# Pacing the bias transfers, moving copies of products, and dividing a tile's four weight differences between GpSimd and VectorE

## What is computed

```python
def swiglu(h, wg, wu, wd):
    return (jax.nn.silu(h @ wg) * (h @ wu)) @ wd

for layer in range(DEPTH):                      # DEPTH = 2, D_MODEL = 1024, D_FF = 2816
    h = rmsnorm(x, ffn_norm_g[layer, 0])
    x = x + 0.5 * swiglu(h, ffn_w_gate[layer, 0], ffn_w_up[layer, 0], ffn_w_down[layer, 0])
    h = rmsnorm(x, mix_norm_g[layer])
    x = x + (gla_ssd_mixer(h, ...) if layer % 2 == 0 else dsa_mixer(h, ..., rel_bias))
    h = rmsnorm(x, ffn_norm_g[layer, 1])
    x = x + 0.5 * swiglu(h, ffn_w_gate[layer, 1], ffn_w_up[layer, 1], ffn_w_down[layer, 1])
return rmsnorm(x, final_norm_g)

# dsa_mixer: score[q, s] = sum over 16 heads of relu(q_idx . k_idx) * w_idx; the top 128 keys are kept;
# logits = q . kv / sqrt(128) + rel_bias[t5_bucket(distance)]; softmax; times kv; out projections
```

## Time and profile before

| | us |
|---|---|
| median of 3 runs (2090.89 to 2091.29) | 2090.96 |
| the profiled execution | 2087.45 |
| its span | 2085.6 |

### The profile page before, as it was taken

How to read it: one execution, slowest core, us unless ns; L and a number is a source line. 1 busy time by engine, 2 the same in 40 slices (tenths; PEclk the granted TensorE clock), 3 DMA queues, 4 the chain that set the end, 5 groups by cost and what they waited for, 6 DMA issues and landing times.

```text
span 2085.6 us, 34512 instructions
## 1 busy us (share of the span) xinstructions
PE 2036.5 (98%) x13775; PEld 1775.9 (85%) x13775; DVE 1558.3 (75%) x2293; ACT 1017.7 (49%) x1597; POOL 537.0 (26%) x431
## 2 busy tenths in 40 slices
PE   7999999999999999999999999999699999999998
PEld 6899998788888887999998899999565678999997
DVE  7777776595777898777776877776479857877775
ACT  5444444453445455444445544444267755544444
POOL 0334330001000002333420333342217412334330
PEclk9999999999999999999999999999899999999999
DMA  5333334332253423333323333334910112333332
GB/s 154 93 110 102 97 105 106 91 93 72 61 142 92 91 82 92 111 92 110 104 85 98 105 108 92 111 102 87 156 42 20 42 56 86 102 112 92 102 91 71
DMA packets 325284, 196.06 MB, mean 94 GB/s; under 512 B 14891, under 2 KB 317110, under 8 KB 325126
## 3 DMA queue, kind: packets, MB, share of 16 engines
q1 hardware_dynamic: 322502, 184.21, 30.5%
q0 software_dynamic: 2624, 9.67, 3.2%
HBM read 191.07 MB, written 2.79 MB: 93 GB/s over the span
## 4 chain that ended last, share of the span: by engine, by line
PE 63%; DVE 5%; DMA 2%; issue 2%; POOL 2%; ACT 1%; DVEq 0%; ACTq 0%; POOLq 0%
PE ps L1993 9%; PE ps L1995 9%; PE ps L1994 9%; PE ps L2058 4%; PE ps L2057 4%; PE ps L2059 4%; PE ps L1872 3%; PE ps L1871 3%; PE ps L1873 3%; DMA w_raw<-in_ffn_w_down 2%; PE ps L2565 1%; PE ps L2536 1%; POOL index_scores L541 1%; PE ps L2515 1%; PE ps L2078 1%
## 5 line engine op out<-in xcount | busy, mean ns | idle before, releaser
L1027 DVE TENSOR_TENSOR w_lo<-w_raw,w_hi 128x1024 fp32r<-128x1024 f32 (+1 forms) x351 | 425.7, 1213 | 72.3 <-ACT w_hi L563 72.2
L563 ACT ACTIVATE w_hi<-w_raw 128x1024 fp32r<-128x1024 f32 (+1 forms) x351 | 361.6, 1033 | 229.3 <-PE ps L1873 110.0
L472 POOL TENSOR_TENSOR sq<-w_raw 128x512 f32<-128x512 f32 x72 | 96.6, 1342 | 953.0 <-DMA w_raw<-in_ffn_w_up 923.5
L1995 PE MATMUL ps<-h_hi,w_lo 128*128 128x256 f32 x864 | 244.5, 283 | 0.0
L1993 PE MATMUL ps<-h_hi,w_hi 128*128 128x256 f32 x864 | 244.2, 283 | 0.0
L2057 PE MATMUL ps<-act_hi,w_hi 128*128 128x512 f32 x512 | 200.0, 391 | 0.0
L2058 PE MATMUL ps<-act_lo,w_hi 128*128 128x512 f32 x512 | 200.0, 391 | 0.0
L2059 PE MATMUL ps<-act_hi,w_lo 128*128 128x512 f32 x512 | 199.2, 389 | 0.0
L1993 PE MATMUL ps<-s_hi,mix_hi 128*128 128x256 f32 x576 | 164.4, 285 | 10.9 <-issue 8.2
L1993 PEld LDWEIGHTS ps<-h_hi,w_hi 128*128 128x128 f32 x864 | 165.6, 192 | 2.7
L1995 PEld LDWEIGHTS ps<-h_hi,w_lo 128*128 128x128 f32 x864 | 165.6, 192 | 0.0
(11 more groups left out here) (409 smaller groups left out, 5367.3 us busy)
## 6 DMA issues: line engine op xcount, KB each, us to landing
w_raw<-in_ffn_w_gate SPq DMA_DIRECT2D x88, 512.0 KB, 3.8
w_raw<-in_ffn_w_up SPq DMA_DIRECT2D x88, 512.0 KB, 3.8
w_raw<-in_ffn_w_down SPq DMA_DIRECT2D x64, 512.0 KB, 3.4
w_raw<-in_hy_w_in SPq DMA_DIRECT2D x44, 512.0 KB, 3.8
w_raw<-in_ffn_w_down SPq DMA_DIRECT2D x32, 384.0 KB, 3.5
w_raw<-in_hy_w_out SPq DMA_DIRECT2D x16, 512.0 KB, 3.9
acum_rows<-acum_scratch POOLq DMA_DIRECT2D x4, 1024.0 KB, 10.5
bias_rows<-line_scratch POOLq DMA_DIRECT2D x8, 512.0 KB, 24.0
```

The costliest lines, as they stand in the source:

```text
L563: act.activation(w_hi[:, s, 0:width[n]], w_raw[:, s, 0:width[n]], ACT.Copy).then_inc(hi_ready, 1)
L1027: dve.tensor_tensor(w_lo[:, s, 0:width[n]], w_raw[:, s, 0:width[n]], w_hi[:, s, 0:width[n]].bitcast(F32), ALU.subtract).then_inc(lo_ready, 1)
L1995: mm = pe.matmul(dst, wl, rh[:, k, :], start=False, stop=k == 3, skip_group_check=True)
```

## The change

Four edits. On GpSimd, `weight_sums` keeps the first two differences of a tile; the two that depend on them are made by VectorE in the new `last_weight_sums`, called for tile 4 after `scaled(1)` and for tile f + 1 after `product(f - 1)`. In mix1 the causal mask is made first, and bias transfer j waits until PE has finished unit `UB["mix1"] - 2 + j` by count: the first for down unit 5 (of 0 to 7), the second and third for 6 and 7, the others for mix1's units 0 to 4. On ScalarE, `keep(f, 0)` moves ahead of `s_high(3)`, `act_high` and `t_high` in tile 4, and ahead of `act_high` in tile 21. In ffn0 alone, `rms_out` and `silu(0)` on ScalarE and `scaled(0)` on VectorE move forward, the first ahead of the eight scaled copies of x and `scaled(0)` ahead of `h_sums`.

```diff
@@ gpsimd, weight_sums and mix1
                 pool.tensor_tensor(up[:, 0:HC], up[:, HC:UC], up[:, 0:HC], ALU.subtract).then_inc(t_made, 1)
-                pool.wait_ge(t_made, 4 * k + 1)
-                pool.tensor_tensor(mix_raw[:, HC:2 * HC], up[:, HC:UC], mix_raw[:, 0:HC], ALU.subtract).then_inc(t_made, 1)
-                pool.wait_ge(t_made, 4 * k + 3)
-                pool.tensor_tensor(mix_raw[:, 2 * HC:3 * HC], gate[:, HC:UC], mix_raw[:, HC:2 * HC], ALU.subtract).then_inc(t_made, 1)
...
-                for j, p0 in enumerate(range(0, P, SKEW)):
-                    lines = bass.AP(tensor=line_dram.tensor, offset=P - 1 - p0, ap=[[LINE - 1, SKEW], [SKEW * LINE, AH], [1, TOK]])
-                    pool.dma_start(bias_rows[p0:p0 + SKEW, :, :], lines).then_inc(pool_landed, 16)
-                pool.dma_start(w_uv_sb[:, :, :], a["dsa_w_uv"][0].rearrange("h c d -> c h d")).then_inc(pool_landed, 16)
                 pool.memset(causal_neg[:, :], 0.0).then_inc(a_cneg, 1)
                 pool.wait_ge(a_cneg, 1)
                 pool.affine_select(out=causal_neg[:, :], in_=causal_neg[:, :], compare_op=ALU.is_ge, fill=MASKED,
                                    base=0, pattern=[[-1, P]], channel_multiplier=1).then_inc(a_cneg, 1)
+                for j, p0 in enumerate(range(0, P, SKEW)):
+                    pool.wait_ge(unit_used, UB["mix1"] - 2 + j)
+                    lines = bass.AP(tensor=line_dram.tensor, offset=P - 1 - p0, ap=[[LINE - 1, SKEW], [SKEW * LINE, AH], [1, TOK]])
+                    pool.dma_start(bias_rows[p0:p0 + SKEW, :, :], lines).then_inc(pool_landed, 16)
+                pool.dma_start(w_uv_sb[:, :, :], a["dsa_w_uv"][0].rearrange("h c d -> c h d")).then_inc(pool_landed, 16)
                 pool.wait_ge(a_cneg, 2)
@@ scalar, ffn
                 act.wait_ge(x_upd, XB[st])
+                if st == STAGES[0]:
+                    rms_out(st)
                 for k in range(KT):
                     act.activation(s_raw[:, k, :], x[:, k, :], ACT.Copy, scale=gains[:, GAIN[st] + k:GAIN[st] + k + 1]).then_inc(s_hi_ready, 1)
                 produce_hi(n + 4)
-                rms_out(st)
+                if st == STAGES[0]:
+                    silu(0)
+                else:
+                    rms_out(st)
                 s_high(0)
                 s_high(1)
-                silu(0)
+                if st != STAGES[0]:
+                    silu(0)
...
+                    produce_hi(nxt_unit)
                     if f == PLAIN:
+                        keep(f, 0)
                         s_high(3)
-                    produce_hi(nxt_unit)
+                    elif f - 1 == LAST + 4:
+                        keep(f, 0)
                     act_high(f - 1)
                     if f < FT - 1:
                         t_high(f + 1)
-                    keep(f, 0)
+                    if f != PLAIN and f - 1 != LAST + 4:
+                        keep(f, 0)
@@ vector, ffn
+                def last_weight_sums(f):
+                    u, k = gate_unit(st, f), kb + f - PLAIN
+                    gate, up = w_raw[:, u % SLOTS, :], w_raw[:, (u + 1) % SLOTS, :]
+                    dve.wait_ge(t_made, 4 * k + 2)
+                    dve.tensor_tensor(mix_raw[:, HC:2 * HC], up[:, HC:UC], mix_raw[:, 0:HC], ALU.subtract).then_inc(t_made, 1)
+                    dve.wait_ge(t_made, 4 * k + 3)
+                    dve.tensor_tensor(mix_raw[:, 2 * HC:3 * HC], gate[:, HC:UC], mix_raw[:, HC:2 * HC], ALU.subtract).then_inc(t_made, 1)
...
+                if st == STAGES[0]:
+                    scaled(0)
                 h_sums()
                 produce_lo(n + 4)
                 s_low(0)
-                scaled(0)
+                if st != STAGES[0]:
+                    scaled(0)
...
                 scaled(1)
+                last_weight_sums(PLAIN)
                 product(1)
...
                     product(f - 1)
+                    if f < FT - 1:
+                        last_weight_sums(f + 1)
```

## The result

| | before | after |
|---|---|---|
| median, us | 2091.02 (2090.89 to 2091.29, 4 runs) | 2056.2 (2054.79 to 2056.34, 4 runs) |
| ratio to before | 1 | 0.983, 95% interval 0.9815 to 0.9849 |
| profiled execution, us | 2087.45 (span 2085.6, clock 0.994) | 2056.34 (span 2054.5, clock 1.000) |
| PE busy, us | 2036.5 (98%) | 2029.2 (99%) |
| VectorE busy, us | 1558.3 (75%) | 1555.1 (76%) |

The change is faster, by 34.8 us between the medians and by 31.1 us between the two profiled executions; the forecast was 25.75.

What follows compares the result with a forecast made beforehand. TensorE was taken as the bound, so gains lie only where it waits. Terms -22.25 + 5 - 3.0 - 4.2 - 1.3 = -25.75 us, off the median 2090.96, gave 2065.2 us; range 2057 to 2076.

Steps and rivals of the forecast that it cites:

- the bias additions: GpSimd's 16 causal-mask additions in mix1 end late and delay the weighted sum at L536: +5 us, ends 0 and 10.
- the basis: Whole kernel: the summed gain of 25.75 us, from the profiled 2087.45, was taken off the median 2090.96.
- The tail of ffn2: Last gate row to norm: pacing bias transfers stops them starving down weights, so it runs as in ffn1: -22.25 us.
- rival (a): In mix1 the bias additions are hidden after all and their 5 us fall away: 2059 us; chance 0.22.
- The product copies: ScalarE's earlier copies cut PE's waits at product 3: -3.0 us in tile 21, -4.2 in tile 4.
- the new stall: In tile 4 PE's wait moves from product 3 to product 5: about 1.45 us, in ffn0 1.9.
- The weight differences: FFN tiles: moving two of GpSimd's four differences to VectorE costs 0 for 72 tiles.
- the room: VectorE in a steady FFN tile: 2.5 us of its 3.77 us idle can be used before PE notices.
- ahead of an FFN's first such tile: VectorE waits up to 2.9 us for GpSimd there, but PE wants the queued work later: cost 0.
- Rival (d): VectorE becomes the bound of the FFN tiles, +53 us: 2118; decides from 2.5 us more per tile; chance 0.05.
- The start of ffn0: Moving rms_out and scaled(0) forward ends PE's wait for the gate row: -1.3 us, 3.4 as the far end.

Runs made afterwards that it cites:

- the control: The changed kernel itself, run again unaltered beside the second group of experiments: 2056.30 us, ratio to before 0.9841.
- the burst put back: The changed kernel with all eight bias transfers issued at once again, at the point where they were: 2078.36 us, ratio to before 0.9950.
- the late burst: The changed kernel with all eight bias transfers issued at once, but only when down unit 5 of ffn2 is done: 2063.36 us, ratio to before 0.9870.
- the doubled run: The changed kernel with GpSimd adding the causal mask to the bias twice: 2062.01 us, ratio to before 0.9873.
- four extra operations: The changed kernel with VectorE making the first of its two weight differences four more times per tile: 2161.31 us, ratio to before 1.0344.
- the run with pacing alone: The kernel before with only the paced bias transfers, placed behind the mask: 2067.99 us, ratio to before 0.9904.
- both undone: The changed kernel with product copies at their old places and all four differences on GpSimd: 2067.26 us, ratio to before 0.9905.
- the copies old: The changed kernel with the copies of products 0 and 1 back at their old places: 2066.61 us, ratio to before 0.9895.

## Why the prediction was off by 9 us

The changed kernel took 9.0 us less than forecast. By the two profiled executions, 4.3 us lie in one term, the bias additions, and 1.1 in the FFNs; the other 3.65 lie in the basis on which the sum was made. The 1.1 is itself a balance: the half clock at ffn0's start was gone (1.5 us, which the control didn't repeat), while the wait for the first norm came 1.3 us later in this execution.

**The tail of ffn2** (-22.25): right. 22.26 us by the start of the row L1065 (L1058), and the burst put back costs them again. Half way between, the late burst shows that the spacing was needed and not only the delay.

**The bias additions** (+5): the mis-sized term and the step that failed; about 0.7 us was lost in mix1, rival (a). The 16 additions were put at 14.5 us and took 9.97. The start was right within 2 us: taken from after's clock, which is 30 us earlier, 1549.9 was to be some 1519, and it was 1517.5. Wrong was the value between the ends: I took the median of a stretch in which each operation met others on VectorE, 0.91 us, and got 0.62. The range of 449 to 1437 ns was a range over neighbours, and the new neighbours were other ones. That a late start of L536 is paid was right (6.0 of 7.6 us in the doubled run). The Trainium skill ("DMA: Bandwidth & Descriptors", Anatomy of one DMA) would have had the additions hidden, and they were, but not for its reason: by its fit 512 KB take an estimated 3.2 us, while w_uv took 8.3 and the bias transfers 11.4 at the median.

**The product copies** (-3.0 and -4.2): the sizes came out, -3.5 at tile 21 and about -4.1 at tile 4 in the profiled executions, and the new stall nearly (1.25 us in ffn1 to ffn3 and 1.67 in ffn0, for 1.45 and 1.9). But at tile 4 the sum came out by luck: 2.0 us in ffn0, with its half clock, 1.5 in ffn1, where the copy had waited for GpSimd, and only 0.3 and 0.4 in ffn2 and ffn3. And the gain doesn't belong to the copies alone: with the differences left on GpSimd the same move gains 2.1 us in all.

**The weight differences** (0): right for the steady tile, and right in each of its rows (0.69 for 1.67, 0.69 for 1.00) but for the room, 1.8 us for 2.5: of VectorE's idle time 1.8 us could not be used, and not 1.26. Wrong as the price of the edit: 8.9 us with the copies moved, 0.7 without. The reasoning that failed is "ahead of an FFN's first such tile" it costs 0. I asked whether VectorE's new work was late for PE, and not what GpSimd's last difference would hold up with the copy moved. The high part of the combinations was in the very queue that I moved the copy past in tile 4; in tile 5 it stayed ahead of the copy, and the moved copy made its weights later. The forecast summed the two edits as if each were alone, and its sum came near the measured one only because the change held both. The Trainium skill ("SBUF — State Buffer", Who interferes with whom) has it that the pair of ports is held for a whole instruction; the 1.67 that returned in some tiles with four extra operations agrees. Rival (d) lay nearer than its 2.5 us said: it needs 1.8 more per tile.

**The start of ffn0** (-1.3): right, 1.27 us in the gap and 1.5 between medians.

**The basis** (3.5 us between profile and median): the prediction took the gain off the median and assumed that it is the same from both. What it skipped is why they differ. The stalls of tile 4 cost the clock in some profiles and not in others: ffn0 alone in the profile before, ffn0 and ffn1 in the run with pacing alone and in the one with both undone, ffn0, ffn2 and ffn3 with the copies old. The stretches are 3 to 7 us long. The profile before was then a lucky one, and a shorter stall gains more at the median than in it. The mean granted clock, which is on record for the executions without a profile too, shows this for the clock as a whole: of 32 executions of the kernel before, the 8 at 0.994 took 2086.9 us on average, the 18 at 0.993 took 2089.0, the 5 at 0.992 took 2090.4, and the one at 0.991 took 2092.6. A thousandth of the clock is an estimated 2.1 us (a thousandth of the span), so the scatter of 2085.4 to 2092.6 us goes with the clock; the profiled execution, 2087.45, had 0.994. The changed kernel, with 0.999 or 1.000 in all nine, scatters from 2054.8 to 2057.4. In which stage the clock fell, an execution without a profile doesn't say. The profile before has half clock in the tail of ffn2 as well, for 17 us, and five executions with the burst put back scatter over 2.5 us, four with pacing alone over 2.1; so that it is tile 4 is argued from the traces and not shown.

## What to carry to other kernels

When a stall of the bounding engine is removed by moving an instruction ahead in a queue, list what now runs later behind it, which requests and producers follow from that, and who waits for them in the next tile; two edits that each gain little may be one gain of 11 us. Space a burst of transfers by the consumer's progress: delaying it alone moves part of the cost to the next consumer (7 of 22 us here). And where a profiled time differs from the median, look for the difference in the trace and in the granted clocks before building a sum on it.

## What the runs showed of the hardware

- The granted clock after one and the same stall is not fixed. A gap of 1.8 us at product 3 of tile 4 was followed by 0.50 in ffn2 and ffn3 in one run and in ffn1 in another; the gap of 2.1 us at the start of ffn0 was followed by it in the control and not in the profile after. The gaps of 1.25 us at product 5 were never followed by it in the profiles of this case.
- A burst starves the weights out of proportion. The queues of the kernel before from 1440 to 1492 us (packets, MB, share of 16 engines; q0 carries the bias and w_uv, q1 the weights):

```profile
q0 software_dynamic: 1296, 4.72, 69.9%
q1 hardware_dynamic: 5196, 1.90, 23.4%
```

  Bias and w_uv moved 4.72 MB in packets of 3.6 KB on average, the weights 1.90 MB in packets of 366 bytes, so the queue with the large packets got three times the engines' time. The Trainium skill ("DMA: Bandwidth & Descriptors", Queues, rings and completion order) says that an engine takes turns between queues at the granularity of packets; the shares agree in kind, though no run here varied the size of a packet, and whether the page and the profile count the same thing as a packet isn't shown.
